# Sorting the experts by count on the chip, and pairing a much used expert with a little used one (96 and 32 rows)

## The reference, cut to what matters

```python
def route_mix(t):                                   # t: (tokens, 1024)
    p_grp = softmax(t @ w_grp)                      # 4 groups of 8 experts
    g_sel, g_w = argmax(p_grp), max(p_grp)
    le_g = (t @ w_exp).reshape(-1, 4, 8)[row, g_sel]
    top_v, top_i = top_k(softmax(le_g), 2)          # 2 experts of that group
    top_v = top_v / sum(top_v)
    combine = ...                                   # (tokens, 32), two entries not 0 a row
    hid = einsum('nd,edf->nef', t, w_ein)           # w_ein: (32, 1024, 512)
    a, b = split(hid, 2, axis=-1)
    act = silu(a) * b * combine[..., None]
    return einsum('nef,efd->nd', act, w_eout)       # w_eout: (32, 256, 1024)
```

## Time and profile before

| | |
|---|---|
| median of 3 runs | 906.89 us (905.81 to 906.90) |
| profiled execution, its own time | 910.62 us |
| profiled execution, its span from first to last instruction | 908.8 us |
| TensorE matmul busy | 748.5 us, 82% |
| TensorE weight load busy | 404.8 us, 45% |
| VectorE busy | 264.8 us, 29% |
| ScalarE busy | 163.4 us, 18% |
| GpSimd busy | 81.5 us, 9% |
| DMA moved | 238.57 MB, mean 263 GB/s |
| mean granted clock of TensorE | 0.910 of full speed |

### The profile page before, as it was taken

How to read it: one execution, slowest core, us unless ns; L and a number is a source line. 1 busy time by engine, 2 the same in 40 slices (tenths; PEclk the granted TensorE clock), 3 DMA queues, 4 the chain that set the end, 5 groups by cost and what they waited for, 6 DMA issues and landing times.

```text
span 908.8 us, 10592 instructions
## 1 busy us (share of the span) xinstructions
PE 748.5 (82%) x3868; PEld 404.8 (45%) x3868; DVE 264.8 (29%) x796; ACT 163.4 (18%) x401; POOL 81.5 (9%) x119
## 2 busy tenths in 40 slices
PE   2999999999999876877789995469978869688634
PEld 2636666555666552434357674333322323222212
DVE  0224323012000696655513214731110111101026
ACT  2012443111000562222210011101110101101002
POOL 0000000023000243000000000110110010110100
PEclk9999999999999899787979997659998999999766
DMA  9958667452450392799989704217999999998151
GB/s 360 399 199 314 237 247 286 173 229 93 160 211 0 135 375 99 256 393 350 353 359 424 316 0 185 58 33 301 425 423 424 421 424 422 425 420 334 61 118 58
DMA packets 51369, 238.57 MB, mean 263 GB/s; under 512 B 8930, under 2 KB 17122, under 8 KB 39090
## 3 DMA queue, kind: packets, MB, share of 16 engines
q1 hardware_dynamic: 42834, 223.93, 62.9%
q0 software_dynamic: 6176, 11.83, 3.8%
q10 hardware_dynamic: 2304, 2.10, 0.7%
HBM read 236.43 MB, written 18.09 MB: 280 GB/s over the span
## 4 chain that ended last, share of the span: by engine, by line
PE 67%; DMA 18%; DVE 9%; issue 3%; ACT 1%; SPq 1%; POOL 0%; POOLq 0%; DVEq 0%; ACTq 0%
PE bank L484 15%; DMA arena<-in_w_ein 15%; PE bank L845 8%; PE bank L457 6%; PE bank L778 4%; PE bank L787 4%; PE bank L865 4%; PE bank L440 2%; PE bank L527 2%; PE bank L738 2%; PE bank L681 2%; PE bank L492 2%; DMA arena<-in_w 1%; PE bank L704 1%; DMA arena<-y_rows 1%
## 5 line engine op out<-in xcount | busy, mean ns | idle before, releaser
L845 PE MATMUL bank<-arena 128*64 128x512 f32 x544 | 138.0, 666 | 33.3 <-DMA arena<-in_w_ein 31.4
L484 PE MATMUL bank<-arena 128*128 128x320 f32 x512 | 141.7, 433 | 0.0
L484 PEld LDWEIGHTS bank<-arena 128*128 128x128 f32 x512 | 95.7, 189 | 45.3 <-issue 6.4
L845 PEld LDWEIGHTS bank<-arena 128*64 128x64 f32 x544 | 42.1, 152 | 118.2 <-issue 84.4
L865 PE MATMUL bank<-arena 128*64 128x512 f32 x272 | 62.1, 598 | 1.4 <-issue 1.4
L1635 DVE COPY arena<-bank 128x512 f32<-128x512 f32 x17 | 11.8, 691 | 162.3 <-PE bank L834 162.3
L457 PE MATMUL bank<-arena 128*128 128x512 f32 x128 | 56.8, 594 | 0.0
L1099 ACT ACTIVATE arena<-bank 128x256 f32<-128x256 f32 x17 | 6.5, 385 | 180.1 <-PE bank L845 180.1
L1761 POOL DMA_INDIRECT y_rows<-arena,rows_of_slots_out x17 | 17.1, 1004 | 231.7 <-DVE arena L1649 231.7
L787 PE MATMUL bank<-arena 128*128 128x320 f32 x128 | 34.8, 432 | 1.5 <-DVE arena L1487 1.5
L457 PEld LDWEIGHTS bank<-arena 128*128 128x128 f32 x128 | 23.4, 187 | 28.5 <-issue 28.3
(11 more groups left out here) (313 smaller groups left out, 889.7 us busy)
## 6 DMA issues: line engine op xcount, KB each, us to landing
arena<-in_w_ein SPq DMA_DIRECT2D x16, 4096.0 KB, 34.2
arena<-in_w_eout SPq DMA_DIRECT2D x16, 2048.0 KB, 24.8
arena<-in_w_ada SPq DMA_DIRECT2D x12, 2048.0 KB, 8.8
arena<-in_w_in SPq DMA_DIRECT2D x10, 2048.0 KB, 10.0
arena<-in_k_pages SPq DMA_DIRECT2D x64, 320.0 KB, 6.5
arena<-in_v_pages SPq DMA_DIRECT2D x64, 320.0 KB, 10.0
arena<-in_cmp_pages SPq DMA_DIRECT2D x48, 128.0 KB, 9.3
arena<-in_win SPq DMA_DIRECT2D x16, 256.0 KB, 5.3
```

The costliest lines, as they stand in the source:

```text
L484: m = mm(banks[c % 4][:, 0:N], ring[q][:, k, P * (c % 4):P * (c % 4 + 1)], hT[:, k, :], start=(k == 0), stop=(k == KD - 1))
L845: m = mm(banks[2 + p % 2][CAP * e:CAP * (e + 1), :], xeT[p % 2][:, k, CAP * e:CAP * (e + 1)], wi2[p % 3][:, e, k, :], start=(k == 0), stop ...
```

## The change

Experts are sorted by their counts on the chip. The first six (FIXED) stay as they are: pairs 0 to 2, whose weights are loaded before the routing is known. The other 26 (FREE_E) are ranked: rank r from 0 to 12 gets pair 3 + r and 96 slots (HEAVY), rank r from 13 to 25 gets pair 28 - r and 32 slots. So pair 3 holds the most and the least used of the 26.

- VectorE: new instructions between `cnt` and the tables. `key` orders by count and, in a tie, by number; `beaten` compares all 26 with all 26; its sum is `rank`; from it come `put` (first slot of an expert) and `room` (its slots). The four instructions that counted extra tiles (L1574, L1576) are replaced by a subtraction, two integer instructions and a copy. Copying `pos` and computing `over` are no longer linked.
- VectorE, behind the tables: `order`, the numbers of the experts by rank, with the new semaphore `s_ord`. The list `extra` is now made after the first `rows_out(0)`, before the rest of the pairs.
- SyncE: waits for `s_ord`; for each pair from 3 on it reads two expert numbers into registers and issues two DMAs for `w_ein` (2 MB each) and two for `w_eout` (1 MB each), where it issued one each.
- TensorE: for pairs 3 to 15 a step has three matmuls in place of two: rows 0 to 63 and 64 to 95 with the much used expert's matrix, rows 96 to 127 with the other's. Pairs 0 to 2 and extra pairs have two of 64 as before.
- Constants: two more blocks of 32 columns (C_PUT, C_ROOM). GpSimd: two semaphores are merged into one; the waits mean the same.

```diff
+            sp.wait_ge(s_ord, 1)
             for p in range(3, PAIRS):
+                of = [sp.value_load(order[0:1, r:r + 1], min_val=0, max_val=E - 1) for r in (p - 3, FREE_E + 2 - p)]
                 sp.wait_ge(s_hd, p - 2)
-                pair_in(p)
+                for u in range(2):
+                    sp.dma_start(wi2[p % 3][:, u].rearrange("p k n -> p (k n)"),
+                                 w_ein[bass.ds(of[u], 1), :, :].rearrange("o p n -> (o p) n")).then_inc(s_wi[p % 3], 16)
                 sp.wait_ge(s_od, 2 * (p - 2))
-                pair_out(p)
+                for u in range(2):
+                    sp.dma_start(wo2[p % 3][:, u].rearrange("p k n -> p (k n)"),
+                                 w_eout[bass.ds(of[u], 1), :, :].rearrange("o p n -> (o p) n")).then_inc(s_wo2[p % 3], 16)
...
+            def tiles_of(p):
+
+                if 3 <= p < PAIRS:
+                    return [(0, 64, 0), (64, 32, 0), (HEAVY, 32, 1)]
+                return [(0, CAP, 0), (CAP, CAP, 1)]
+
...
                 for k in range(KD):
-                    for e in range(2):
-                        m = mm(banks[2 + p % 2][CAP * e:CAP * (e + 1), :], xeT[p % 2][:, k, CAP * e:CAP * (e + 1)],
-                               wi2[p % 3][:, e, k, :], start=(k == 0), stop=(k == KD - 1))
+                    for r, n, e in tiles_of(p):
+                        m = mm(banks[2 + p % 2][r:r + n, :], xeT[p % 2][:, k, r:r + n], wi2[p % 3][:, e, k, :],
+                               start=(k == 0), stop=(k == KD - 1))
...
-            link(ve.tensor_copy(pos[R], banks[1][R, 0:4 * E].rearrange("p (t e) -> p t e", e=E)))
+            put, room = cst[R, C_PUT:C_PUT + E], cst[R, C_ROOM:C_ROOM + E]
...
             link(ve.tensor_copy(cnt[R], banks[1][R, 4 * E:5 * E]))
-
-            link(ve.tensor_scalar(more[R], cnt[R], CAP + 0.5, None, ALU.is_ge))
-            for n in range(2, N // CAP):
-                link(ve.scalar_tensor_tensor(more[R], cnt[R], n * CAP + 0.5, more[R], ALU.is_ge, ALU.add))
+            link(ve.scalar_tensor_tensor(key[R], cnt[R], float(E), cst[R, C_E:C_E + E], ALU.mult, ALU.subtract))
+            link(ve.tensor_tensor(beaten, key[R, FIXED:E].unsqueeze(1).to_broadcast(every),
+                                  key[R, FIXED:E].unsqueeze(2).to_broadcast(every), ALU.is_gt))
+            link(ve.tensor_reduce(rank[R], beaten, AX, ALU.add))
+            ve.tensor_scalar(less[R], rank[R], FREE_E / 2 - 0.5, None, ALU.is_ge)
+            ve.tensor_scalar(up[R], rank[R], float(P), 3.0 * P, ALU.mult, ALU.add)
+            link(ve.tensor_scalar(put[:, FIXED:], rank[R], -float(P), (FREE_E + 2.0) * P, ALU.mult, ALU.add))
+            ve.tensor_tensor(up[R], up[R], put[:, FIXED:], ALU.min)
+            link(ve.tensor_scalar(room[:, FIXED:], less[R], 32.0 - HEAVY, float(HEAVY), ALU.mult, ALU.add))
+            ve.tensor_copy(pos[R], banks[1][R, 0:4 * E].rearrange("p (t e) -> p t e", e=E))
+            link(ve.scalar_tensor_tensor(put[:, FIXED:], less[R], float(HEAVY), up[R], ALU.mult, ALU.add))
+            wholei = whole_i[:, :]
+            link(ve.tensor_tensor(more[R], cnt[R], room, ALU.subtract))
+            link(ve.tensor_scalar(wholei, more[R], 0.0, CAP - 1.0, ALU.max, ALU.add))
+            link(ve.tensor_scalar(wholei, wholei, 6, None, ALU.logical_shift_right))
+            link(ve.tensor_copy(more[R], wholei))
...
-            link(ve.tensor_scalar(over[R], pos[R], CAP - 0.5, None, ALU.is_ge))
+            ve.scalar_tensor_tensor(over[R], pos[R], 0.5, room.unsqueeze(1).to_broadcast([RT, 4, E]), ALU.add, ALU.is_ge)
+            link(ve.tensor_tensor(far[R], far[R], room, ALU.subtract))
+            link(ve.tensor_tensor(far[R], far[R], put, ALU.subtract))
...
+            link(ve.tensor_tensor(same, cst[0:1, C_E:C_E + FREE_E].unsqueeze(2).to_broadcast(wide1),
+                                  rank[0:1].unsqueeze(1).to_broadcast(wide1), ALU.is_equal))
+            link(ve.tensor_tensor(same, same, cst[0:1, C_E + FIXED:C_E + E].unsqueeze(1).to_broadcast(wide1), ALU.mult))
+            link(ve.tensor_reduce(key[0:1, 0:FREE_E], same, AX, ALU.add))
+            ve.tensor_copy(order[:, :], key[0:1, 0:FREE_E]).then_inc(s_ord, 1)
...
+            rows_out(0)
+
             which, tab = big[0:1].rearrange("p a b c -> p (a b c)"), at(rt + 1500, 16)
             for k in range(EXTRA):
...
-            rows_out(0)
             ve.wait_ge(s_wt, 1)
```

More of the change, by code:

```diff
@@ L50 @@
 PAIRS = E // 2
+FIXED = 6
+FREE_E = E - FIXED
+HEAVY = 96
 ALLP = PAIRS + EXTRA // 2
@@ L64 @@
 C_E = C_LT + 128
-C_HALF = C_E + E
+C_PUT = C_E + E
+C_ROOM = C_PUT + E
+C_HALF = C_ROOM + E
 C_ROW = C_HALF + 2
@@ L90, in build @@
         row_out = ctx.enter_context(nc.sbuf_tensor("rows_of_slots_out", [P, ALLP], I32))
+        order = ctx.enter_context(nc.sbuf_tensor("experts_by_count", [1, FREE_E], I32))
+        whole_i = ctx.enter_context(nc.sbuf_tensor("whole_tiles", [RT, E], I32))
         extra = ctx.enter_context(nc.sbuf_tensor("extra_tiles", [1, 1 + EXTRA], I32))
@@ L275, in build @@
         s_m, s_pos, s_flag = sem("chosen"), sem("positions"), sem("extra_tiles_ready")
+        s_ord = sem("experts_sorted")
         s_ht, s_hr = sem("h_rows_turned"), sem("h_rows_ready")
@@ L284, in build @@
         s_ch = sem("vector_chain")
[L285 removed]
+        s_z, s_y = sem("gpsimd_zeros_written"), sem("y_written")
         s_ms, s_rms = sem("mean_square"), sem("root_mean_square")
@@ L863, in pair_output @@
                     for j in range(2):
-                        for e in range(2):
-                            m = mm(banks[6 + half][CAP * e:CAP * (e + 1), :], actT[:, p % 2, j, CAP * e:CAP * (e + 1)],
+                        for r, n, e in tiles_of(p):
+                            m = mm(banks[6 + half][r:r + n, :], actT[:, p % 2, j, r:r + n],
                                    wo2[p % 3][:, e, j, 512 * half:512 * (half + 1)], start=(j == 0), stop=(j == 1))
@@ L1585, in _ @@
             link(ve.tensor_tensor(far[R], end, more[R], ALU.subtract))
-            link(ve.tensor_scalar(far[R], far[R], float(CAP), float(CAP * (E - 1)), ALU.mult, ALU.add))
-            link(ve.tensor_tensor(far[R], far[R], cst[R, C_E:C_E + E], ALU.subtract))
-            link(ve.tensor_scalar(over[R], pos[R], CAP - 0.5, None, ALU.is_ge))
+            link(ve.tensor_scalar(far[R], far[R], float(CAP), float(CAP * E), ALU.mult, ALU.add))
+            ve.scalar_tensor_tensor(over[R], pos[R], 0.5, room.unsqueeze(1).to_broadcast([RT, 4, E]), ALU.add, ALU.is_ge)
+            link(ve.tensor_tensor(far[R], far[R], room, ALU.subtract))
+            link(ve.tensor_tensor(far[R], far[R], put, ALU.subtract))
             link(ve.tensor_tensor(over[R], over[R], far[R].unsqueeze(1).to_broadcast([RT, 4, E]), ALU.mult))
-            link(ve.tensor_tensor(pos[R], pos[R], cst[R, C_E:C_E + E].unsqueeze(1).to_broadcast([RT, 4, E]), ALU.add))
+            link(ve.tensor_tensor(pos[R], pos[R], put.unsqueeze(1).to_broadcast([RT, 4, E]), ALU.add))
             link(ve.tensor_tensor(pos[R], pos[R], over[R], ALU.add))
@@ L1620, in _ @@
             ve.tensor_copy(wtab, banks[3][:, ALLP:2 * ALLP]).then_inc(s_wt, 1)
[L1622 to L1628, removed]
+            same = cst[0:1, C_TRI:C_TRI + FREE_E * FREE_E].rearrange("p (r e) -> p r e", e=FREE_E)
+            wide1 = [1, FREE_E, FREE_E]
+            link(ve.tensor_tensor(same, cst[0:1, C_E:C_E + FREE_E].unsqueeze(2).to_broadcast(wide1),
[3 more added lines that the diff above has]
+            ve.tensor_copy(order[:, :], key[0:1, 0:FREE_E]).then_inc(s_ord, 1)
             def rows_out(p):
@@ L1651, in _ @@
             rows_out(0)
+            which, tab = big[0:1].rearrange("p a b c -> p (a b c)"), at(rt + 1500, 16)
+            for k in range(EXTRA):
+                link(ve.tensor_scalar(which[:, 0:E], ends[1][0:1, 16:48], k + 0.5, None, ALU.is_le))
+                link(ve.tensor_reduce(tab[0:1, 1 + k:2 + k], which[:, 0:E], AX, ALU.add))
+            link(ve.tensor_scalar(tab[0:1, 1:1 + EXTRA], tab[0:1, 1:1 + EXTRA], E - 1.0, None, ALU.min))
+            link(ve.tensor_copy(tab[0:1, 0:1], ends[1][0:1, 47:48]))
+            ve.tensor_copy(extra[:, :], tab[0:1, 0:1 + EXTRA]).then_inc(s_flag, 1)
             ve.wait_ge(s_wt, 1)
@@ L1711, in smp_zeros @@
             def smp_zeros(k):
-                po.memset(qz[k], 0.0).then_inc(z_q0, 1)
-                po.wait_ge(z_q0, k + 1)
+                po.memset(qz[k], 0.0).then_inc(s_z, 1)
+                po.wait_ge(s_z, k + 2)
             def smp_queries(i):
@@ L1746, in _ @@
             for k in range(3):
-                po.memset(xeS[k], 0.0).then_inc(s_xz, 1)
-            po.wait_ge(s_xz, 3)
+                po.memset(xeS[k], 0.0).then_inc(s_z, 1)
+            po.wait_ge(s_z, 6)
             po.wait_ge(s_rows, 1)
@@ L1810, in constants @@
     c[:, C_LT:C_LT + P] = r[:, None] < r[None, :]
-    c[:, C_E:C_E + E] = CAP * np.arange(E)
+    c[:, C_E:C_E + E] = np.arange(E)
```

(2 more changed lines are left out.)

10 lines of the change are left out of this document (6 added, 4 removed).

## The result

The changed kernel takes 1013.4 us (median of 4 runs, 1010.5 to 1017.2), the one before 906.9. The ratio is 1.115, 95% interval 1.110 to 1.120. The forecast was 884.7, faster. The profiled execution took 1010.5 us with a span of 1008.7.

What follows compares the result with a forecast made beforehand. Weight transfers were taken to set the pace, 15.6 us a pair against TensorE's 12.0. Span 908.8 + 1.7 (sort) - 23.9 (extra pair) = 886.6, with 1.8 around it 888.4, median 3.7 lower: 884.7 us, range 881 to 891.

Steps and rivals of the forecast that it cites:

- The step that failed: TensorE, pairs 3 to 15: a round of three column tiles takes the same 0.44 us as two; cost nothing.
- The cover: Expert stage: DMA's 15.6 us a pair against TensorE's 12.0 hides 3.6 us of extra TensorE work up to pair 15.
- second rival: Three tiles in pairs 3 to 15 do not overlap and cost 1.5 of two; 910.4 us, slower; chance 0.05.
- factor 1.3: Rival 1, TensorE: three tiles overlap only in part, so the stage's end pays 4.3 us; 889.0 us; chance 0.09.
- The rule of the Trainium skill: TensorE column tiles: by it a round of three costs 1.26 times as much, making the sum 3.7 us worse.
- The extra pair: End of the expert stage: the seventeenth pair, needed for expert 27's 67 rows, goes; gain 23.9 us.
- The sort: VectorE's chain ahead of the gathers grows by 1.7 us, and all behind it moves by this.
- The stall: VectorE's sort: two-input instructions or a reduction beside GpSimd's memsets might stall, up to 1.4 us more; not taken.
- Order table and extra table: VectorE: order table in the old place of the extra table, which moves later; cost nothing, cover 4 us.
- Loads by number: SyncE, pairs 3 on: register loads and split weight loads cost nothing; bound 1 us.
- rival 3: Weights come slower in 2 MB pieces from scattered places, 5.7 us; 890.4 us; chance 0.05.
- Rival 4: The extra pair stays, through other inputs or a count that does not fit; 908.6 us; chance 0.02.

Runs made afterwards that it cites:

- run 3: Changed kernel, same matmuls, but all steps of the 64-wide tile first, then all steps of the two 32-wide ones: 979.9 us, ratio 1.080.
- run 1: Changed kernel with the 96 rows as three tiles of 32, so four tiles of 32 a step: 890.6 us, repeated 887.9 us, ratio 0.978.
- run 5: Changed kernel with three tiles a step, all 32 wide, rows 64 to 95 not computed: 887.0 us, ratio 0.977.
- run 8: Changed kernel with 64 and 64 rows in every pair, keeping sort and loads by number, extra pair back: 912.7 us, ratio 1.0082 to the kernel before.
- run 10: Kernel of run 1, with SyncE reading the next pair's expert numbers ahead of its wait for the output: 887.5 us, ratio 0.978.
- run 7: Kernel before with four tiles of 32 in place of two of 64 in pairs 3 to 15: 906.2 us, ratio 0.999.
- run 9: Kernel before with each weight load from pair 3 on split in two at fixed addresses, no register loads: ratio 1.002.
- run 11: Kernel before with loads split at fixed addresses, but in the expert order that the sort gives: ratio 1.001.
- run 12: Kernel of run 1, with SyncE issuing w_ein of pair p before w_eout of pair p - 1: 877.2 us, ratio 0.968.

## Why the prediction was wrong

**The step that failed** is "Three in a round must then fit in the same 0.44. Cost nothing", with "I take the factor 1". The factor is 15.95 / 7.09 = 2.25. The cover went with it: I had set TensorE's 12.0 us a pair against DMA's 15.6, and it was 25.2, so TensorE and no longer the loads set the pace. My second rival had the right mechanism, tiles that do not overlap, and priced it at 1.5, counting three tiles at half a round each. But a tile by itself takes a whole round, 0.43 us (run 3), and I did not ask which two could still lie together. With the 64-wide tile apart, a step is two rounds for it and two for the other two, four in place of two, and 0.13 us for each of the two changes. Had I priced it so, the rival would have read 12.0 + 8.9 + 4.4 = 25.3 us a pair, where 25.2 was measured.

The account: `hidden(3)` to `hidden(15)` 110.8 longer, from there to the end without an extra pair 37.4 (975.52 - 938.11) where run 1's trace has 22.1 (853.29 - 831.21), so 15.3; sort 1.5; extra pair -24.1. That is 103.5. The medians are 106.5 apart and the two traced executions 99.9; this difference is not placed. The stages around the experts vary by some us: in the trace of the changed kernel the sort began 2.5 us earlier, and from the signal to the end it was 33.2 us where it was 35.0.

**Why the rows misled.** L440 and L738 showed four tiles side by side, and I wrote that no row has unequal widths, then chose by L440 all the same. The trace of before had the answer nearer. L738, my "factor 1.3", changes width with L742 every 16 records (TensorE's timeline of the kernel before):

```profile
383.26 1.07 PE L738 MATMUL bank<-arena 128*32 128x256 f32 x16
384.26 0.66 PE L742 MATMUL bank<-arena 128*64 128x128 f32 x8
384.85 1.07 PE L738 MATMUL bank<-arena 128*32 128x256 f32 x16
```

Start to start the 16 narrow records take 1.00 us where four rounds of half of 0.43 are 0.86, the 8 wide ones 0.59 where four of a quarter are 0.43. The 0.14 and 0.16 too much agree with the 0.13 for a change of width above; no run tests it at this place. I read a change of width as bad packing, and so used as an upper bound a row that could not bound anything: both groups fill all columns, so they had no room to overlap. The bound should have been the sum of the tiles one after another, three times two rounds in place of two, a factor of 3.0: no row excluded it.

**The rule of the Trainium skill** that I weighed ("TensorE: Matmul & The Clock Gate", section "Measured speedup vs the span model", three column tiles 2.38 times one) was no guide to this either: for three tiles of one width run 5 shows no loss at all (7.07 us for 16 rounds, as with four), and for mixed widths the time was that of two groups one after the other (15.95 us).

**The extra pair**, priced at 23.9: from `hidden(15)` to the signal 46.16 us before (873.78 - 827.62) and 22.08 in run 1, gain 24.1. Right.

**The sort**, 1.7: 1.5, right. The stall went as I had chosen: the comparison ran wholly beside the memsets (577.25 to 579.98) and took 0.86 us, the speed expected, and the first `tensor_scalar` came behind them. This agrees with the Trainium skill, "SBUF — State Buffer", section "Who interferes with whom". Of the reduction's 0.85 us only the first 0.23 lay beside the memsets, so it tells little.

**Order table and extra table**, nothing: in the changed kernel the first `hidden` started 0.87 us behind its turned rows, as before (0.88).

**Loads by number**, nothing: the stretch is 2.3 to 3.3 us longer than the 223.5 of the kernel before. In all four kernels with loads by number that keep TensorE short and the old order of issue (runs 1, 5, 8, 10) the stretch takes 225.8 to 226.8 us; in the four that load in any other way (before, 7, 9, 11) 223.0 to 223.8. Splitting, register loads ahead of the issue, and scattered addresses are each ruled out (runs 9, 10 and 11, one traced execution each). Left are the addressing by register itself and the uneven gathers of sorted pairs; between these it stays open.

The kept traces narrow it. Some 2 us are there when `hidden(6)` starts, the first that waits for weights for long: 78.5 to 79.3 us behind `hidden(0)` in the kernels with loads by number, 76.2 to 77.6 in the others. The DMA engines were not slower until then. They had moved more, 26.9 to 27.1 MB where it was 25.9 to 26.4. Sorted pairs are full at the front: pairs 3 to 8 hold 292 rows where they held 148, and at 4 KB a row that is 0.6 MB more to gather and some 0.2 MB more to scatter (an estimate from the counts), near 2 us at 425 GB/s. So the uneven gathers can account for this part. From `hidden(6)` to `hidden(15)` it is 147.3 to 147.6 us where it was 146.1 to 146.7, and in its first 130 us the engines move 419 to 421 GB/s where they moved 423 or 424. In that part the sorted pairs have fewer rows, not more, so their bytes do not explain it.

**The sum** without the failed step, corrected by 2.3: 906.9 - 24.1 + 1.5 + 2.3 = 886.6, and run 1 repeated gave 887.9. Of the 5.7 us of rival 3, 2.3 to 3.3 came, and not for the reason that it gives: pieces of 2 MB and scattered addresses cost nothing that runs 9 and 11 show. Rival 4 did not happen.

## What to carry to other kernels

Column tiles lay side by side only where they had one width (float32, 128 rows, 512 columns moved): cut everything to the narrowest width in use, even where it doubles the instructions. An overlap that no row shows is to be bounded by no overlap at all, tile after tile, and it is worth asking which instructions could still pair up. Where loads set the pace, look at the order in which freed buffers are asked for: run 12 gained 10.7 us by it. By the traces the first idle gap and whatever stands in front of the last load are both on the path.

## What the runs showed of the hardware

- Two matmuls of unequal column width never overlapped: 64 with 32 (15.90 us), 96 with 32 (16.03), 64 with two of 32 (15.95), against 7.07 for three or four of 32 and 7.09 for two of 64. A 64-wide tile by itself takes 0.43 us a round, as much as two or four equal tiles together. A change of width costs some 0.13 us on top (run 3 against the changed kernel).
- Tiles that read one matrix at once are as fast as tiles on different ones: 7.07 us with three of four on one matrix (run 1), 7.09 with two of two on different ones.
- With loads by a number in a register and sorted pairs, pair 15 started 225.8 to 226.8 us behind pair 0, else 223.0 to 223.8. Splitting the loads, scattered addresses and the time of the register loads are excluded as causes; register addressing and the uneven gathers are not taken apart.
